# Neighbourhood attention with tokens ordered by grid column: each query tile meets 256 of the 512 keys

## The reference

```python
C_WIN_R = 8; C_WIN_C = 16; GRID_W = 64
def natten_indices(s):
    rows = s // GRID_W; wr = min(C_WIN_R, rows)
    t = jnp.arange(s); r = t // GRID_W; c = t % GRID_W
    rs = jnp.clip(r - wr // 2, 0, rows - wr)
    cs = jnp.clip(c - C_WIN_C // 2, 0, GRID_W - C_WIN_C)
    kr = rs[:, None, None] + jnp.arange(wr)[None, :, None]
    kc = cs[:, None, None] + jnp.arange(C_WIN_C)[None, None, :]
    ...                                   # idx, and the offsets off_r, off_c into the bias table
# natten_branch: bias = rpb[:, off_r, off_c]
#   softmax(q . k[idx] / 8 + bias) . v[idx]
```

## Time and profile before

| what | value |
|---|---|
| median of 3 runs | 2649.4 us (2648.29 to 2651.61) |
| the profiled execution | 2648.02 us, its span 2645.9 us |
| busy in the span: PE, DVE, ACT, POOL | 99%, 56%, 43%, 2% |
| neighbourhood stage, layer 1 | first scores 821.1 us, last value product 926.8 us |
| the same, layer 2 | 1970.2 us to 2075.9 us |
| granted TensorE clock, mean | 0.997 of full |

### The profile page before, as it was taken

The page is one execution under the profiler, slowest core; times in us unless marked ns, Lnnn a source line. Parts: engine busy times, 40 slices in busy tenths (PEclk is TensorE's granted clock), DMA queues, the critical chain, the costliest instruction groups (busy, mean ns, idle before and its releaser), DMA issues.

```text
span 2645.9 us, 34045 instructions
## 1 busy us (share of the span) xinstructions
PE 2606.2 (99%) x13218; PEld 2178.7 (82%) x13218; DVE 1486.6 (56%) x2770; ACT 1126.6 (43%) x1929; POOL 41.4 (2%) x67
## 2 busy tenths in 40 slices
PE   8998999999999999999999999999999999999998
PEld 6887878888888888888888788888888887888887
DVE  6756667554545558554444586544456486544445
ACT  3436354333645647232222344335546374322223
POOL 0000000000000000000000000000001000000000
PEclk9999999999999999999999999999999999999999
DMA  4220223123124321233333231232134221333332
GB/s 150 81 64 29 80 57 104 49 83 96 51 65 91 78 86 57 74 108 96 96 97 99 79 94 56 72 96 70 49 94 78 88 74 64 97 97 101 96 96 88
DMA packets 118352, 216.98 MB, mean 82 GB/s; under 512 B 14177, under 2 KB 21601, under 8 KB 118193
## 3 DMA queue, kind: packets, MB, share of 16 engines
q1 hardware_dynamic: 114240, 201.63, 24.6%
q0 software_dynamic: 3808, 12.92, 3.1%
q10 hardware_dynamic: 144, 0.26, 0.0%
HBM read 212.69 MB, written 2.10 MB: 81 GB/s over the span
## 4 chain that ended last, share of the span: by engine, by line
PE 93%; DVE 4%; ACT 1%; issue 1%; DMA 0%; SPq 0%; ACTq 0%; DVEq 0%
PE bank L574 44%; PE bank L577 31%; PE bank L728 5%; PE bank L717 3%; PE bank L697 2%; PE bank L698 2%; PE bank L757 1%; PE bank L774 1%; PE bank L618 1%; PE bank L811 1%; DVE hL L1592 0%; DVE wL L1489 0%; PE bank L749 0%; DMA wraw<-in_w_in_dram 0%; PE bank L632 0%
## 5 line engine op out<-in xcount | busy, mean ns | idle before, releaser
L1489 DVE TENSOR_TENSOR wL<-wraw,wH 128x1024 fp32r<-128x1024 f32 (+1 forms) x388 | 459.9, 1185 | 642.5 <-ACT wH L969 640.8
L969 ACT ACTIVATE wH<-wraw 128x1024 fp32r<-128x1024 f32 (+1 forms) x388 | 398.3, 1026 | 880.3 <-PE bank L574 469.1
L574 PE MATMUL bank<-wH,hH 128*128 128x512 f32 (+1 forms) x1248 | 500.2, 401 | 0.7 <-DVE wL L1489 0.7
L574 PE MATMUL bank<-wH,hL 128*128 128x512 f32 (+1 forms) x1248 | 478.4, 383 | 0.0
L574 PE MATMUL bank<-wL,hH 128*128 128x512 f32 (+1 forms) x1248 | 478.1, 383 | 0.0
L577 PE MATMUL bank<-hH,wH 128*128 128x512 f32 x1208 | 474.7, 393 | 1.6 <-ACT hH L1037 0.9
L577 PE MATMUL bank<-hH,wL 128*128 128x512 f32 x1208 | 470.8, 390 | 0.0
L577 PE MATMUL bank<-hL,wH 128*128 128x512 f32 x1208 | 470.8, 390 | 0.0
L574 PEld LDWEIGHTS bank<-wH,hH 128*128 128x128 f32 x1248 | 235.8, 189 | 52.0 <-issue 3.8
L574 PEld LDWEIGHTS bank<-wH,hL 128*128 128x128 f32 x1248 | 235.8, 189 | 48.6 <-issue 3.8
L574 PEld LDWEIGHTS bank<-wL,hH 128*128 128x128 f32 x1248 | 235.4, 189 | 47.8
(11 more groups left out here) (320 smaller groups left out, 2831.4 us busy)
## 6 DMA issues: line engine op xcount, KB each, us to landing
wraw<-in_w_in_dram SPq DMA_DIRECT2D x180, 512.0 KB, 3.5
wraw<-in_w_ffn_down_dram SPq DMA_DIRECT2D x44, 512.0 KB, 3.4
wraw<-in_w_ffn_gate_dram SPq DMA_DIRECT2D x40, 512.0 KB, 3.5
wraw<-in_w_ffn_up_dram SPq DMA_DIRECT2D x40, 512.0 KB, 3.5
wraw<-in_w_out_dram SPq DMA_DIRECT2D x24, 512.0 KB, 3.5
tab<-in_rpb_rev_dram POOLq DMA_DIRECT2D x32, 224.0 KB, 6.3
wraw<-in_w_up_a_dram SPq DMA_DIRECT2D x8, 512.0 KB, 3.4
wraw<-in_w_up_b_dram SPq DMA_DIRECT2D x8, 512.0 KB, 3.4
```

The lines of the kernel that those rows point to most:

```text
L574: mm = pe.matmul(bank[t][:, 0:b.cols], act_part[:, k, t * P:(t + 1) * P], w_part[:, kk, :], start=first, stop=last)
L969: A(wH[:, u % W_SLOTS, 0:width], wraw[:, u % RAW_SLOTS, 0:width], ACT.Copy).then_inc(S["w_hi"], 1)
L1489: V.tensor_tensor(wL[:, u % W_SLOTS, 0:width], wraw[:, u % RAW_SLOTS, 0:width], wH[:, u % W_SLOTS, 0:width].bitcast(F32), ALU.subtract).th ...
```

## The change

Inside the neighbourhood stage the tokens are ordered by grid column. A tile of 128 queries is then 16 columns by 8 rows, and the windows of its 16 columns lie within 32 columns, 256 keys that are contiguous in the new order. An item has 256 keys in place of 512, and with them scores, sum with the table, exponential, transposes, copy and value product.

The order is made in these places. Queries and keys are put in column order by the split into high and low parts, which reads each row with a step of 64 elements (`by_column`). The values are put in order through DRAM on POOL's queue: after CV is evacuated, `v1` is written to a tensor in DRAM (1 MB) and read back in seven pieces of 256 KB, one for each start at a multiple of 8 columns, into `v1` and `v2`. The output goes back to natural order in `hi_chunks` and `lo_chunks`, which write with a step of 64 elements. The bias of a head is one load of 265 elements per partition into a single buffer, issued when the table of the head before is made, and DVE makes three tables of 256 elements from it, reading with a step of 31. The mask is loaded by three small DMAs on POOL's queue at the start. Alibi tables for the next stage wait until all items of this one are done.

```diff
+GRID_R, GRID_C = 8, 64
+WIN_C = 32
+NAT_KEYS = GRID_R * WIN_C
+NAT_C0 = (0, 8, 24, 32)
+NAT_TYPE = (0, 1, 1, 2)
+NAT_SHIFT = (0, 8, 16)
...
 def nat_items():
-    return [dict(kind="nat", h=h, t=t, comp=0, kmax=SEQ, head=h, q=(h // 2, h % 2), k=(h // 2, h % 2),
-                 v=(h * DH, DH), y=h * DH) for h in range(HEADS) for t in range(NT)]
+    return [dict(kind="nat", h=h, t=t, comp=0, kmax=NAT_KEYS, key0=GRID_R * NAT_C0[t], head=h, q=(h // 2, h % 2),
+                 k=(h // 2, h % 2), v=(h * DH, DH), y=h * DH) for h in range(HEADS) for t in range(NT)]
+def by_column(z):
+    return z.rearrange("p (r c) -> p c r", c=GRID_C)
+def column_rows(z):
+    return z.rearrange("p (c r) -> p c r", r=GRID_R)
...
             zeros(None)
+            for j, t in enumerate((0, 1, 3)):
+                src = bass.AP(tensor=a["nat_mask"].tensor, offset=16 * t * DH + DH - WIN_C - NAT_C0[t],
+                              ap=[[DH, 16], [0, GRID_R], [1, WIN_C]])
+                pool.dma_start(nat_mask[:, j, :], src).then_inc(S["mask_dma"], 16)
...
                 zero_halves("U01")
+                cv = by_name[(l + 1, "CV")]
+                for t in range(NT):
+                    pool.wait_ge(free[t], cv.nth[t] + 1)
+                pool.dma_start(v_rows.rearrange("(t p) n -> p t n", p=P), v1).then_inc(S["v_out"], 16)
+                pool.wait_ge(S["v_out"], 16 * (l + 1))
+                for j in range(7):
+                    src = bass.AP(tensor=v_rows.tensor, offset=8 * j * SEQ,
+                                  ap=[[SEQ, 16], [GRID_C * SEQ, GRID_R], [1, SEQ]])
+                    pool.dma_start((v2 if j % 2 else v1)[:, j // 2, :], src).then_inc(S["v_moved"], 16)
+                pool.wait_ge(S["mx_done"], gqa0 + 1)
                 for h in range(HEADS):
-                    if h == 2:
+                    if h == 1:
                         zero_halves("U11")
-
-                    pool.wait_ge(S["mx_done"], gqa0 + 1 if h < 2 else nat0 + 4 * (h - 1))
-                    for half in range(2):
-                        off = l * (RPB_LEN + 2 * RPB_PAD) + RPB_PAD + RPB_LEN - 1 - RPB_HEAD * h - (14 - half) * 31 - 78
-                        src = bass.AP(tensor=a["rpb_rev"].tensor, offset=off, ap=[[1, 64], [31, 14], [1, 64]])
-                        pool.dma_start(tab[64 * half:64 * half + 64, h % 2, :].rearrange("p (e k) -> p e k", e=14),
-                                       src).then_inc(S[f"tab_dma{h % 2}"], 16)
+                    if h:
+                        pool.wait_ge(S["table_ready"], HEADS * l + h)
+                    off = l * (RPB_LEN + 2 * RPB_PAD) + RPB_PAD + RPB_LEN - 1 - RPB_HEAD * h - 14 * 31 - 46
+                    src = bass.AP(tensor=a["rpb_rev"].tensor, offset=off, ap=[[1, 16], [31, GRID_R], [1, BIAS_W]])
+                    pool.dma_start(bias_rows, src).then_inc(S["bias_dma"], 16)
...
+                        keys = slice(it.get("key0", 0), it.get("key0", 0) + kmax)
+                        pe.matmul(dst[:, 0:kmax], q_split[slot][:, tok], k_twice[slot][:, keys], start=True, stop=False)
+                        mm = pe.matmul(dst[:, 0:kmax], q_split[slot][:, tok], k_low[slot][:, keys], start=False,
...
+            def nat_values(t, c):
+                if t in (0, 3):
+                    return v1[:, c + 2 * (t // 3), :]
+                return v2[:, c + t - 1, :]
...
                 evacuated(B("CV")[0])
-                softmax(nat_items(), v1, side_groups(B("G20", "G21"), B("DV")[0]))
+                pe.wait_ge(S["v_moved"], 112 * (l + 1))
+                softmax(nat_items(), None, side_groups(B("G20", "G21"), B("DV")[0]))
...
+                    if columns:
+                        A(by_column(dst[:, k, :]), column_rows(src[:, :]), ACT.Copy).then_inc(S["tp_hi"], 1)
...
+                if items[0]["kind"] == "nat":
+                    A(column_rows(q_split[g % 2][r, :]), by_column(q[r, qi, :]), ACT.Copy)
+                    A(column_rows(k_twice[g % 2][0:DH, :]), by_column(k[r, ki, :]), ACT.Copy)
+                    A(column_rows(k_twice[g % 2][DH:P, :]), by_column(k[r, ki, :]), ACT.Copy).then_inc(S["hi_done"], 1)
+                    return
...
+                    if columns:
+                        V.tensor_tensor(by_column(lo[:, k, :]), column_rows(src[:, :]),
+                                        by_column(hi[:, k, :].bitcast(F32)), ALU.subtract).then_inc(S["tp_free"], 1)
+                        continue
...
+                if items[0]["kind"] == "nat":
+                    V.tensor_tensor(column_rows(q_split[g % 2][other, :]), by_column(q[r, qi, :]),
+                                    column_rows(q_split[g % 2][r, :].bitcast(F32)), ALU.subtract)
+                    V.tensor_tensor(column_rows(k_low[g % 2][r, :]), by_column(k[r, ki, :]),
+                                    column_rows(k_twice[g % 2][r, :].bitcast(F32)), ALU.subtract).then_inc(
+                        S["split_done"], 1)
+                    return
...
+            def nat_table(h, kinds):
+                if kinds[0] == 0:
+                    dve.wait_ge(S["bias_dma"], n("bias", 16))
+                for j in kinds:
+                    bias = bass.AP(tensor=bias_rows.tensor, offset=bias_rows.offset + NAT_SHIFT[j],
+                                   ap=[list(bias_rows.ap[0]), [1, WIN_C], [31, GRID_R]])
+                    ins = V.scalar_tensor_tensor(out=column_rows(nat_tables[h % 2][j]), in0=bias, scalar=1.0 / SCALE,
+                                                 in1=nat_mask[:, j, :].unsqueeze(2).to_broadcast([P, WIN_C, GRID_R]),
+                                                 op0=ALU.mult, op1=ALU.add)
+                if kinds[-1] == 2:
+                    ins.then_inc(S["table_ready"], 1)
+                    dve.wait_ge(S["table_ready"], n("table_ready"))
...
+                            if kind == "nat":
+                                table = nat_tables[it["h"] % 2][NAT_TYPE[it["t"]]][:, ::-1]
...
                     if kind == "nat" and s % NT == 3 and s + 1 < len(items):
-                        for half in range(2):
-                            nat_table(s // NT + 1, half)
+                        nat_table(s // NT + 1, (0, 1, 2))
```

More of the change, by code:

```diff
@@ L51 @@
 TABW = 896
+GRID_R, GRID_C = 8, 64
[4 more added lines that the diff above has]
+NAT_SHIFT = (0, 8, 16)
+BIAS0 = 2 * 3 * NAT_KEYS
+BIAS_W = 31 * (GRID_R - 1) + 48
 RPB_PAD = 64
@@ L728, in softmax @@
                             mm = pe.matmul(bank[PV][:, 0:w], sbufPT[:, y % 2, c * P:(c + 1) * P],
-                                           v[:, c, c0:c0 + w], start=c == 0, stop=c == nk - 1)
+                                           (nat_values(it["t"], c) if kind == "nat" else v[:, c, :])[:, c0:c0 + w],
+                                           start=c == 0, stop=c == nk - 1)
                         mm.then_inc(S["pv_done"], 1)
+            def nat_values(t, c):
+                if t in (0, 3):
+                    return v1[:, c + 2 * (t // 3), :]
+                return v2[:, c + t - 1, :]
             def evacuated(b):
@@ L1029, in last_rows, with hi_chunks @@
                         done()
-            def hi_chunks(chunks, dst, scale, banks=None):
+            def hi_chunks(chunks, dst, scale, banks=None, columns=False):
                 for k in chunks if isinstance(chunks, tuple) else range(chunks):
@@ L1036, in hi_chunks @@
                     src = bank[banks[k] if banks else SC + i % TR_BANKS]
-                    A(dst[:, k, :], src[:, :], ACT.Copy, scale=scale(k)).then_inc(S["tp_hi"], 1)
+                    if columns:
+                        A(by_column(dst[:, k, :]), column_rows(src[:, :]), ACT.Copy).then_inc(S["tp_hi"], 1)
+                    else:
+                        A(dst[:, k, :], src[:, :], ACT.Copy, scale=scale(k)).then_inc(S["tp_hi"], 1)
             def normed(l, name, gain, evac=None, between=None):
@@ L1073, in split_rows @@
                     act.wait_ge(S["sc_done"], n.at("items") - len(items) + NT * (g - 1))
+                if items[0]["kind"] == "nat":
[3 more added lines that the diff above has]
+                    return
                 ins = A(q_split[g % 2][r, :], q[r, qi, :], ACT.Copy,
-                        scale=1.0 if items[0]["kind"] in ("nat", "diff") else SCALE)
+                        scale=1.0 if items[0]["kind"] == "diff" else SCALE)
                 if not keeps_k(items, g):
@@ L1406, in _ @@
                 dense(L, "DV", start=1, stop=3)
-                hi_chunks(4, yH, lambda k: 1.0)
+                hi_chunks(4, yH, None, columns=True)
                 dense(L, "DV", copy_to(lambda t: v2[:, t, :]), start=3)
@@ L1584, in last_rows, with lo_chunks @@
                 each(3)
-            def lo_chunks(chunks, hi, lo, scale, banks=None):
+            def lo_chunks(chunks, hi, lo, scale, banks=None, columns=False):
                 for k in chunks if isinstance(chunks, tuple) else range(chunks):
@@ L1712, in softmax @@
```

(9 more changed lines are left out.)

26 lines of the change are left out of this document (15 added, 11 removed).

## The result

The changed kernel takes 2630.9 us (median of 4 runs, 2629.5 to 2632.6) against 2648.9 for the kernel before on the same chip: a ratio of 0.9935, 95% interval 0.9922 to 0.9948. That is 18 us gained where the forecast was 48. The sign and the range hold; the size is that of the first rival, strided reads at about one and a half times and more. The profiled execution took 2631.2 us, span 2629.4.

What follows compares the result with a forecast made beforehand. PE's own work was taken to bound the kernel. From the profiled 2648.0 us, minus 54.4 saved plus 6.6 of stalls gave 2600.2; with 1.4 for the median 2601.6, stated as 2601, range 2590 to 2644.

Steps and rivals of the forecast that it cites:

- the first rival: Strided reads in the neighbourhood stage cost up to two times: 2639 us at two, 2620 at one and a half; chance 0.35.
- PE's own saving: Neighbourhood stage: a PE step falls from 3.18 to 2.33 us with fewer keys, 54.4 us over 64 items.
- The third rival: Scores with fewer columns are no cheaper, each matmul needing its own weight load: 14 us lost, 2615 us; chance 0.04.
- The hidden parts: Values through DRAM, bias, alibi and mask loads cost nothing; the strided output at most 0.5 us a layer.
- The output's split on DVE: Under DV's last unit: 2.48 us for four chunks beside 5.5 us of matmuls; twice the price would just touch that cover.
- The move of the values: 1 MB out to DRAM and 1.75 MB back on POOL's queue: some 30 to 40 us, hidden before the stage.
- The limit in the stage: ACT and DVE work per head takes 9.88 us against PE's 9.32, stalling PE 3.3 us a layer, 6.6 in all.
- the ring: Chain of dependent ACT and DVE work, from a step 0 copy to step 4's copy, run six times a stage: 9.88 us.
- the two returns through DVE: Reciprocal, scaling and table sum in steps 3 and 4 of the chain, priced 0.61 + 0.35 and 0.61 + 0.43 us.
- the fourth rival: The ACT and DVE chain never shows, its links being a little shorter: 2595 us; its chance lies within 0.50 for 2590 to 2612.
- The price of a stepped read: Strided ACT and DVE reads in the stage, taken at a price of one; each further time adds 3.15 us per chain.
- The other side: Second rival: strided reads above 2.27 times make the kernel slower, about 2677 us at three; chance 0.11 including other endings above 2644.

## Why the prediction was right and wrong

**PE's own saving: right.** 54.4 forecast, 54.2 measured with all reads plain; the step is 2.30 where 2.33 was summed. The third rival, scores no cheaper at 256 columns, is out by the pair at 0.32.

**The hidden parts: right.** No wait for the values' way through DRAM, the bias loads or the alibi loads. The output's split on DVE became 4.1 us where 2.48 stood, as allowed, and making it 2.5 again changed nothing. The move of the values was overestimated, 30 to 40 us for at most 17, at no cost.

**The limit in the stage: right in place, some 0.7 us too long.** PE's waits lie in each head's last step, for L1170's copy and L1762's scaling, as foretold. The working put the ring at 9.88 with plain reads, so that it should have shown by 6.6 us; it doesn't show. The version with the waits filled shows a whole ring at full clock, without tanh, in two rows of ACT's timeline, each the first row copy of its head:

```profile
867.89 1.14 ACT L1131 ACTIVATE yL<-set 64x512 fp32r<-64x512 f32 x1
...
879.49 1.14 ACT L1131 ACTIVATE yH<-set 64x512 fp32r<-64x512 f32 x1
```

That is 11.60 us. The prediction's terms with the measured reads put in give 9.88 + 1.43 (rows on ACT, 3.37 for 1.94) + 0.66 (rows on DVE, 2.12 for 1.46) + 0.40 (tables, 1.74 for 1.34) = 12.37. Of the 0.77 too much, 0.52 are in the two returns through DVE: reciprocal, scaling and sum were priced 0.61 + 0.35 and 0.61 + 0.43, and took 0.74 (876.56 to 877.30 above). The 0.61 was the distance from the reciprocal to the sum of 512 columns, a gap of 0.13 in it; ahead of the sum of 256 columns it is 0.40. Another 0.26 are the two copies, priced 0.40 with their gap, which took 0.26 and 0.28 from their start to the next operation (877.39 and 879.21 in that run). So with plain reads the ring is about 9.1, and 8.9 with the 1.12 us that plain tables take for the 1.34 of the prediction, under PE's 9.3: the fourth rival. One premise holds only while the reads are dear: that the ring no longer passes through PE. With plain tables its last copy waits for PE's transposes.

**The price of a stepped read: the step that failed.** It was named as the unknown, bounded by 3.15 us a ring for each further time, and then taken as one. It is 1.8 on ACT, 1.5 on DVE's rows and 1.5 on the tables (627 for 420). The short rows had pointed there: four elements 16 bytes apart took as long as twelve in runs of three, 160 and 162 ns, which the prediction itself read as leaning towards "a price of about two", and then set aside, since fixed costs could do the same on so few. They were the only rows near the question, and the choice of the base case went against them. The first rival had this case, at a chance of 0.35; at 1.5 it gave 2620, and the ring's own formula with the measured reads, 6 x (12.37 - 9.32) - 0.1 = 18.2 a layer, gives 2601.6 - 6.6 + 36.4 = 2631.4.

**That this meets the 2630.9 measured is an accident.** The ring's base was too long by 0.77, worth 9 us over twelve rings (12 x 0.77), and a second cost of 10 us was missing: the clock. The prediction priced PE's idle time as its own length, the second step that failed. With the waits filled the same ring costs 28 us, not 38. Nothing in the rows of before could show it, since PE had no waits there inside the stage.

**The other side.** Slower needed a ring of 13.87; the measured one is 11.6 us at full clock, 12.2 on average. Single heads in which the clock fell took up to 13.4, so that margin was thinner than the prediction said.

What stays open is how PE's idle time must lie for the clock to fall. At one wait of up to 1.1 us a head it held in all twelve rings. In the changed kernel, with two waits a head, 1.4 to 2.2 us together, it fell after eight of twelve, and their size doesn't sort them: after 1.45 us it fell at 888 and not at 839, after 1.83 at 851 and not at 877.

## What to carry to other kernels

When a change swaps dense reads for stepped ones, count the elements that it moves onto a chain that nobody's work hides, and give a step of 16 bytes or more in SBUF one and a half to two times the time until a run says otherwise; better, do the reordering once, in a read from PSUM that happens anyway. When a change shortens the bound engine's work, follow the loop through the other engines around one period and compare it with the new period: here some 37 of 54 us of gain were lost on a loop that the stepped reads made 2.5 us longer, 10 of them by the clock that fell in PE's waits. And take the small rows that answer the question over the argument that they are small.

## What the runs showed of the hardware

- A step in SBUF costs time from 16 bytes on, in reads and in writes, on ACT and DVE (steps of 16, 32, 124 and 256 bytes were measured): reads of 64x512 take 1.12 us for 0.63 on ACT and 1.05 for 0.69 on DVE; written with a step, 128x512 on ACT takes 1.18 for 0.60, and a table on DVE 0.68 where plain is 0.42. A read at 8 bytes is free.
- A step in a read from PSUM is free: at 256 bytes on ACT 600 ns (plain 601), at 32 bytes on ACT 604 and on DVE 684 (plain 684).
- Waits of PE of 1.4 to 2.2 us a head, in a stage otherwise full, brought the granted clock from 1.00 to 0.93 on average, with stretches at the 1.2 GHz level; work of no use in these waits kept it at 1.00 and made the kernel 10 us faster.
